# Attention of a two-layer hybrid trunk: looped jobs with f32 value matmuls against one unrolled pipeline with probabilities in two parts

## What is computed

```
# layer 0: 8 latent heads (mla, 96-dim keys) and 8 forgetting heads (fox, bias F[t] - F[s]), all causal
p = softmax(q @ k.T * scale + bias, masked s <= t);  o = p @ v
# layer 1: dilated heads, 3 groups (d1, d4, d16: window / dilation 128/1, 512/4, 2048/16) x 4 heads
lse_g = logsumexp(logits_g);  o_g = softmax(logits_g) @ v_g
o = sum_g softmax_over_groups(lse_g) * o_g          # the merge
# layer 1: 4 sparse heads, three branches on the same queries
o = gate0 * cmp(63 compressed keys) + gate1 * sel(causal here, top 16 of 16 blocks) + gate2 * win(512 back)
mix = concat(o) @ w_out
```

## Time and profile before

| | us |
|---|---|
| median of 3 runs (3382.21 to 3389.79) | 3389.16 |
| profiled execution: span | 3393.3 |
| its own time beside the span | none is recorded apart; the span stands for it, 4.1 above the median |
| TensorE busy (share of the span) | 3124.6 (92%) |
| VectorE busy | 1348.8 (40%) |
| GpSimd busy | 809.7 (24%) |
| ScalarE busy | 727.8 (21%) |
| mean granted clock of TensorE, of full speed | 0.937 |
| first attention, first score to first output projection | 297.5 to 692.8 |
| second attention | 1991 to 2444.1 |

### The profile page before, as it was taken

The page is one execution under the profiler, slowest core; times in us unless marked ns, Lnnn a source line. Parts: engine busy times, 40 slices in busy tenths (PEclk is TensorE's granted clock), DMA queues, the critical chain, the costliest instruction groups (busy, mean ns, idle before and its releaser), DMA issues.

```text
span 3393.3 us, 46007 instructions
## 1 busy us (share of the span) xinstructions
PE 3124.6 (92%) x14660; PEld 2555.4 (75%) x14660; DVE 1348.8 (40%) x2457; ACT 727.8 (21%) x1197; POOL 809.7 (24%) x466
## 2 busy tenths in 40 slices
PE   8897988898999999999999986688889999999999
PEld 5776888875888888876788875577758888888867
DVE  4634554505222222226433148876443222222254
ACT  2203433313100111113210022233331111111131
POOL 2330021321332332322233202100113233233222
PEclk9998987898999999999999986777799999999999
DMA  4236411100111111110135263344101111111101
GB/s 158 107 118 186 104 47 37 49 31 25 50 45 49 49 44 49 49 56 31 38 117 210 79 163 92 88 102 102 44 25 44 50 49 43 49 49 43 62 32 75
DMA packets 69611, 241.10 MB, mean 71 GB/s; under 512 B 9091, under 2 KB 12675, under 8 KB 68663
## 3 DMA queue, kind: packets, MB, share of 16 engines
q1 hardware_dynamic: 57992, 196.35, 19.4%
q10 hardware_dynamic: 11488, 43.16, 3.3%
HBM read 195.60 MB, written 48.59 MB: 72 GB/s over the span
## 4 chain that ended last, share of the span: by engine, by line
PE 79%; DVE 11%; issue 4%; ACT 3%; DMA 2%; SPq 0%; DVEq 0%; ACTq 0%; POOL 0%; POOLq 0%
PE ACC L895 59%; PE OP L1070 7%; PE ACC L1030 5%; PE TR L1045 4%; PE OP L951 3%; DVE R L1487 2%; DVE T L1510 1%; DVE H L1513 1%; DVE XL L1493 1%; PE TR L1082 1%; DVE T L1535 1%; ACT PT L1293 1%; DVE HL L1538 1%; DMA BIASD<-b_d 1%; ACT T L1267 1%
## 5 line engine op out<-in xcount | busy, mean ns | idle before, releaser
L792 POOL CAST WH<-RAW 128x1024 fp32r<-128x1024 f32 x203 | 215.8, 1063 | 1946.1 <-PE ACC L895 1755.7
L895 PE MATMUL ACC<-XH,WH 128*128 128x512 f32 x1792 | 581.6, 406 | 52.4 <-DVE XL L1493 38.4
L895 PE MATMUL ACC<-XL,WH 128*128 128x512 f32 x1792 | 556.8, 392 | 0.0
L895 PE MATMUL ACC<-XH,WL 128*128 128x512 f32 x1792 | 555.7, 391 | 0.0
L794 POOL TENSOR_TENSOR WL<-RAW,WH 128x1024 fp32r<-128x1024 f32 x203 | 495.4, 2440 | 24.2
L895 PEld LDWEIGHTS ACC<-XH,WH 128*128 128x128 f32 x1792 | 337.9, 190 | 158.8 <-issue 75.9
L895 PEld LDWEIGHTS ACC<-XL,WH 128*128 128x128 f32 x1792 | 338.9, 189 | 71.7
L895 PEld LDWEIGHTS ACC<-XH,WL 128*128 128x128 f32 x1792 | 338.7, 189 | 71.8
L1542 DVE TENSOR_TENSOR M<-M,ACC 128x1024 f32<-128x1024 f32 x128 | 156.3, 1221 | 520.8 <-PE ACC L895 520.8
L895 PE MATMUL ACC<-HH,WH 128*128 128x512 f32 x1024 | 322.2, 396 | 17.0 <-DVE HL L1538 17.0
L1265 ACT ACTIVATE HH<-T 128x1024 fp32r<-128x1024 f32 x64 | 68.0, 1062 | 1168.5 <-DVE T L1535 1168.5
(11 more groups left out here) (188 smaller groups left out, 3339.9 us busy)
## 6 DMA issues: line engine op xcount, KB each, us to landing
RAW<-in_w SPq DMA_DIRECT2D x203, 512.0 KB, 3.2
QK<-y_odds SPq DMA_DIRECT2D x128, 256.0 KB, 5.1
y_odds<-HALVES ACTq DMA_DIRECT2D x16, 1024.0 KB, 5.0
QK<-y_foxs SPq DMA_DIRECT2D x48, 256.0 KB, 5.6
y_foxs<-HALVES ACTq DMA_DIRECT2D x8, 1024.0 KB, 4.7
y_kv<-Q ACTq DMA_DIRECT2D x8, 512.0 KB, 2.6
BIAS<-y_f SPq DMA_DIRECT2D x4, 1024.0 KB, 8.3
y_odd<-HALVES ACTq DMA_DIRECT2D x8, 512.0 KB, 2.6
```

The source lines that it names most:

```text
L792: nc.gpsimd.tensor_copy(WH[:, slot], RAW[:, slot]).then_inc(s_whi, 1)
L895: mm = nc.tensor.matmul(acc[:, h * HALF:(h + 1) * HALF], w(k), x[:, k, h * HALF:(h + 1) * HALF], start=first and k == k0 and w is ws and x ...
```

## The change

The attention of each layer becomes one straight line of steps through all its jobs, without loops: `EVEN_JOBS` (4 fox, 4 mla jobs of two heads) and `ODD_JOBS` (d1, d4, d16, cmp of pair 0, the same of pair 1, then sel, win, sel, win). The lags of two and three steps stay. In it:

- A turned group is made into two fp32r parts. For the first four blocks of a task (kind A) ScalarE copies hi and VectorE subtracts lo from `TR`; for the rest (kind B) ScalarE copies to `PTF` and GpSimd makes hi and lo. `PT` now holds two such parts for a chunk of two tasks (256 queries).
- `VS` holds hi and lo of V side by side, 64 columns each, and is the stationary operand; `PT` moves, 256 queries wide. The result is feature rows of V-hi and V-lo, for four tasks (a half) in one `OP` bank. ScalarE copies the lo rows to `CORR`, VectorE adds them and multiplies by the inverse sums, which a matmul of a broadcast column with the identity has turned into a row (`norm`). Transposes of the output go; GpSimd makes `XH` and `XL` (for sel and win it adds the branches too).
- Dilated heads spread sum and extreme over 64 rows with the same matmul. The merge is 14 pieces, one in each step after the last dilated half.
- Mla heads are padded pairs of the same form; the split of Q and K is four pieces in the steps of blocks 2 to 5 (`split_head`).
- Small tasks (dilated, cmp) have four banks of scores and eight of probabilities, the others two and three.
- Room for this is H's: it is overwritten in attention, stored ahead of the second one (`y_h`, eight stores in the gate stage) and loaded back behind each (`reload_h`). SP and ScalarE wait for all stores of the stage before, ahead of the first job; CMPMASK is loaded first in the second attention. Each head's bias is loaded by itself.

```diff
+EVEN_JOBS = [("fox", p) for p in range(4)] + [("mla", p) for p in range(4)]
+ODD_JOBS = ([(k, 0) for k in DILATED] + [("cmp", 0)] + [(k, 1) for k in DILATED] + [("cmp", 1)]
+            + [("sel", 0), ("win", 0), ("sel", 1), ("win", 1)])
...
+        for s in range(len(ts) + VALUE_LAG + 2 + MERGE_PIECES):
+            st = Phase()
+            st.logits, st.turn, st.values, st.norm, st.out, st.start = get(s), get(s - TURN_LAG), None, None, None, None
+            if st.logits and st.logits.first_of_head and st.logits.e == 0:
+                st.start = st.logits.job
+            ended = get(s - VALUE_LAG)
+            if ended and ended is ended.chunk.tasks[1]:
+                st.values = ended.chunk
+                if ended.chunk.closes:
+                    st.norm = ended.chunk.half
+            st.out = ph.steps[-1].norm if ph.steps else None
+            st.merge = [(p, s - s0) for p, s0 in merging if 0 < s - s0 <= MERGE_PIECES]
+            if st.out and st.out is st.out.job.halves[-1] and st.out.job.kind == "d16":
+                merging.append((st.out.job.pair, s))
+                ph.merged[st.out.job.pair] = st.out.no + 1
+            st.split = None
...
+        def group_free(eng, g):
+            if g.seq > 2:
+                x = pt_groups[g.seq - 3]
+                if x.kind == "A":
+                    eng.wait_ge(s_ptD, x.d)
+                else:
+                    eng.wait_ge(s_ptA, x.a)
...
+                def split_turned(t):
+                    c = t.chunk
+                    m = c.tasks.index(t)
+                    for g in t.groups:
+                        if g.kind != "B":
+                            continue
+                        k0 = t.blocks[0] - c.k0 + g.first
+                        hi, lo = (PT[:, c.buf, hl, k0:k0 + g.n, m * P:(m + 1) * P] for hl in range(2))
+                        src = PTF[:, (g.b - 1) % 2, 0:g.n * P].rearrange("p (k q) -> p k q", q=P)
+                        pool.wait_ge(s_ptA, g.a)
+                        wait(pool, s_pv, c.no - 1)
+                        nc.gpsimd.tensor_copy(hi, src).then_inc(s_pth, 1)
+                        pool.wait_ge(s_pth, g.b)
+                        nc.gpsimd.tensor_tensor(lo, src, hi.bitcast(F32), ALU.subtract).then_inc(s_ptB, 1)
...
+                def spread_sums(h):
+                    c0 = h.tasks[0].col
+                    pool.wait_ge(s_exp, h.tasks[-1].no + 1)
+                    wait(pool, s_nrm, h.no - 1)
+                    nc.gpsimd.tensor_copy(PTF[:, h.no % 2].rearrange("p (t m f) -> p t m f", t=4, m=2),
+                                          NML[:, :, c0:c0 + 4].rearrange("p m t -> p t m").unsqueeze(3)
+                                          .to_broadcast([P, 4, 2, HD])).then_inc(s_rl, 1)
...
+                def values(c):
+                    j, col = c.job, c.c % 2 * 256
+                    pe.wait_ge(s_ptD, c.d)
+                    wait(pe, s_ptB, c.b)
+                    if c.opens:
+                        wait(pe, s_o, c.half.no)
+                    order = sorted(c.keys, key=lambda x: x[1] - x[2])
+                    for n, (k, c0, c1) in enumerate(order):
+                        for hl in range(2):
+                            v, pt = VS[:, j.slot, k, c.e * P:(c.e + 1) * P], PT[:, c.buf, hl, k - c.k0, c0:c1]
+                            if j.kind == "cmp":
+                                v, pt = VCS[:, c.e * P:(c.e + 1) * P], PT[0:HD, c.buf, hl, 0, c0:c1]
+                            mm = nc.tensor.matmul(OP[:, 0, col + c0:col + c1], v, pt,
+                                                  start=c.opens and n == 0 and hl == 0,
+                                                  stop=c.closes and n == len(order) - 1 and hl == 1,
+                                                  skip_group_check=True)
+                    mm.then_inc(s_pv, 1)
...
+                def norm(h):
+                    pe.wait_ge(s_rl, h.rl)
+                    wait(pe, s_o, h.no)
+                    wait(pe, s_cor, h.cor_before)
+                    for m, t in enumerate(h.tasks):
+                        if h.job.kind in DILATED:
+                            rows = PTF[:, h.no % 2, m * P:(m + 1) * P]
+                        else:
+                            rows = RL[:, t.col:t.col + 1].to_broadcast([P, P])
+                        mm = nc.tensor.matmul(OP[:, 1, m * P:(m + 1) * P], rows, IDENT[:], start=True, stop=True)
+                    mm.then_inc(s_nrm, 1)
...
+                def correction(h):
+                    rows, other = rows_of_head(h.e), rows_of_head(1 - h.e)
+                    act.wait_ge(s_pv, h.chunks[1].no + 1)
+                    wait(act, s_o, h.no)
+                    nc.scalar.activation(CORR[rows], OP[other, 0], ACT.Copy).then_inc(s_cor, 1)
+                    if h.job.kind in DILATED:
+                        act.wait_ge(s_nrm, h.no + 1)
+                        if h.job.kind == "d1" and h is h.job.halves[0]:
+                            wait(act, s_ox, h.job.pair)
+                        dst, src = by_token(h, DL[rows, DILATED.index(h.job.kind)], OP[HD:P, 1])
+                        nc.scalar.activation(dst, src, ACT.Copy).then_inc(s_cor, 1)
...
+                def turned(t):
+                    c = t.chunk
+                    m, r = c.tasks.index(t), HD if t.kind == "cmp" else P
+                    for g in t.groups:
+                        act.wait_ge(s_tr, g.seq)
+                        src = TR[0:r, g.ring, 0:g.n * P]
+                        if g.kind == "B":
+                            wait(act, s_ptB, g.b - 2)
+                            nc.scalar.activation(PTF[:, (g.b - 1) % 2, 0:g.n * P], src, ACT.Copy).then_inc(s_ptA, 1)
+                            continue
+                        k0 = t.blocks[0] - c.k0 + g.first
+                        wait(act, s_pv, c.no - 1)
+                        nc.scalar.activation(PT[0:r, c.buf, 0, k0:k0 + g.n, m * P:(m + 1) * P],
+                                             src.rearrange("p (k q) -> p k q", q=P), ACT.Copy).then_inc(s_ptA, 1)
...
+            def reload_h(name, src):
+                end = phases[name].end
+                act.wait_ge(s_tr, end.turned)
+                act.wait_ge(s_ttr, end.tasks)
+                wait(act, s_ptB, end.b)
+                wait(act, s_ops, end.ops)
+                if name == "odd":
+                    act.wait_ge(s_ox, 2)
+                for c in range(DC):
+                    act.dma_start(H[:, c], src[c]).then_inc(s_hre, 16)
...
+                def low_turned(t):
+                    c = t.chunk
+                    m, r = c.tasks.index(t), HD if t.kind == "cmp" else P
+                    for g in t.groups:
+                        if g.kind == "B":
+                            continue
+                        k0 = t.blocks[0] - c.k0 + g.first
+                        hi, lo = (PT[0:r, c.buf, hl, k0:k0 + g.n, m * P:(m + 1) * P] for hl in range(2))
+                        dve.wait_ge(s_ptA, g.a)
+                        V_.tensor_tensor(lo, TR[0:r, g.ring, 0:g.n * P].rearrange("p (k q) -> p k q", q=P),
+                                         hi.bitcast(F32), ALU.subtract).then_inc(s_ptD, 1)
...
+                def outputs(h):
+                    j, rows = h.job, rows_of_head(h.e)
+                    dve.wait_ge(s_cor, h.cor)
+                    if j.kind in DILATED:
+                        g = DILATED.index(j.kind)
+                        if j.kind == "d1" and h is j.halves[0]:
+                            wait(dve, s_ox, j.pair)
+                        dst, src = by_token(h, DU[rows, g], OP[rows, 0])
+                        _, cor = by_token(h, DU[rows, g], CORR[rows])
+                        V_.tensor_tensor(dst, src, cor, ALU.add)
+                        dst, src = by_token(h, DM[g][rows], OP[0:HD, 1])
+                        V_.tensor_copy(dst, src).then_inc(s_o, 1)
+                        return
+                    cols = slice(h.h * HALF, (h.h + 1) * HALF)
+                    dst = XF[rows, j.chunk, cols]
+                    if j.kind in ("sel", "win"):
+                        wait(dve, s_xl, h.xl_before)
+                        dst = O[rows, cols]
+                    if j is ph.jobs[-1] and j.kind == "mla" and h.no % 4 == 0:
+                        dve.wait_ge(s_ops, j.ops[1])
+                    V_.tensor_tensor(dst, OP[rows, 0], CORR[rows], ALU.add).then_inc(s_o1, 1)
+                    dve.wait_ge(s_o1, h.o1)
+                    dve.wait_ge(s_nrm, h.no + 1)
+                    V_.tensor_tensor(dst, dst, OP[rows, 1], ALU.mult).then_inc(s_o, 1)
...
+                def merge(p, k):
+                    n = MERGE_STEPS * p
+                    if k == 1:
+                        dve.wait_ge(s_o, ph.merged[p])
+                        V_.tensor_tensor(DMIN[:], DM[0][:], DM[1][:], ALU.min).then_inc(s_md, 1)
+                    elif k == 2:
+                        dve.wait_ge(s_md, n + 1)
```

(14 more changed lines are left out.)

998 lines of the change are left out of this document (465 added, 533 removed).

## The result

The changed kernel takes 3464.8 us (median of 4 runs, 3462.0 to 3469.4) against 3385.7 of the kernel before (4 runs): **1.0239 times the time, 95% interval 1.0222 to 1.0256, 79 us slower**, where 76 us less were forecast. The profiled span is 3462.3 us. The mean granted clock is 0.938, as before.

What follows compares the result with a forecast made beforehand. Gaps and merges, more than the steady heads, were taken as what could be won: 34.4 us in the first attention and 41.8 in the second, 76.2 off 3393.3, gave 3317.1 us profiled, 3313 as median; range 3224 to 3375.

Steps and rivals of the forecast that it cites:

- their 58 matmuls in 10 us: Large heads: argument against a falling clock, since 61 matmuls in 10 us had shown 1.00 and new heads have 58.
- Work of 16.2 and 0.4 for signals: Fox head: 128 TensorE records take 16.2 us, the many more signals 0.4, within 22.0 us a head.
- Matmuls of 256 columns at 0.112 us: Value matmuls, 256 queries wide: taken at 0.112 us each; at 0.16, 1.5 us more a head.
- Denominators 0.9 a half: New denominator rows on TensorE: 8 f32 matmuls, 16 records a head at 0.112 us; 0.9 us in the tail.
- Place one: T6 behind the next head's L0: TensorE waits 2.3 us for VectorE's low part, queued behind score and output passes.
- Place two: The 16 value matmuls after L2: TensorE waits 2.1 us for ScalarE's copies and GpSimd's cast and subtraction.
- Place three: First values of a head after L4: TensorE waits 1.0 us for VectorE's score pass, outputs and low part.
- the clock falls inside the heads: Rival, 0.12: TensorE's pauses lower the clock, some 11 us more per head at 1.2 GHz; 3389 us and up.
- waits of 0.5 and 1.8: Four d1 tasks: values wait twice for the low part, beside 4.2 us of TensorE work; 6.0 us forecast.
- small tasks win nothing: Rival, 0.18: TensorE stays at 1.2 GHz, 48 tasks take 100 us, both merges show in full; 3361 us.
- the prediction's second way: Merge: VectorE's DL products meet GpSimd's DU products even in pieces, so it costs 25 us; uncontended 15.
- the 5.6 and 11.2 given: First attention's bias load: 5.6 us as it is halved, or 11.2 if the 1.5 MB beside it held it.

Runs made afterwards that it cites:

- run 3: Values four steps behind the scores instead of three, nothing else, against the changed kernel: 3340.6 us, 0.9857 of the kernel before.
- run 4: Changed kernel with 128x512 matmuls of no use ahead of the scores of blocks 0 and 2 in fox and mla heads: 3452.9 us.
- run 11: On run 3, the merge passes work on 8 columns of 1024, leaving nearly all of the merge out; one execution: 3312.4 us.
- run 8: On run 3, one more wait: GpSimd begins its merge products only after VectorE's ten two-input passes: 3328.8 us, 0.9843 of the kernel before.

## Why the prediction was wrong

Its sum against the profile (us):

| term | forecast | measured | off |
|---|---|---|---|
| first score | 292 | 295.97 | +4 |
| first attention, first score to first output matmul (710.56) | 366.4 | 414.6 | +48.2 |
| between the attentions, to the second's first score (2014.47) | 1307.2 | 1303.9 | -3.3 |
| two dilated groups | 152 | 200.4 | +48.4 |
| two compressed jobs and merges | 36 + 44 | 97.9 | +17.9 |
| selected, window, filling and tail | 170.3 | 200.5 | +30.2 |

That is 145 of the 152 us by which the forecast missed; the rest is how the profiled executions stand to the medians (4.1 below the span taken, 2.5 above it measured).

**The large heads, the step that failed: a price list without the clock.** The prediction priced TensorE's work at full clock all through the heads, and took their 58 matmuls in 10 us as the reason. Work of 16.2 and 0.4 for signals: right (16.5 here, 16.9 in run 3). Matmuls of 256 columns at 0.112 us: right in short bursts (eight in 0.88 at 406.30 in the chain), 0.13 in bursts of sixteen (2.08). Denominators 0.9 a half: right at full clock (0.94 at 407.18), 1.78 behind a pause (397.60). Place one 2.3: measured 2.4. Place two 2.1: 7.4 / 4 = 1.85. Place three 1.0: 5.0 / 4 = 1.25. Missed were the transposes of V, which at the start of each pair take place one's buffer and wait 2.9 instead: 6.4 us of waits a head for 5.4. The other 2.55 us are the clock. Two mla heads took 51.1 us (bursts at 601.64 and 652.78 in the chain), 25.6 each for 22.6, at a clock of 0.93. The rival "the clock falls inside the heads" had 0.12, and its price, 11 us for a whole head at 1.2 GHz, was the wrong form of it: the clock fell in short pieces in nearly every head. My argument against it, a mean density of matmuls like that of a window at full clock, says nothing on pauses of 2.4 us between bursts; run 4 is the test of it. That waits of 2.3 us are "far shorter" than those after which the rows showed 0.50 was true, and no evidence that they are harmless. The Trainium skill (TensorE: Matmul & The Clock Gate, HAM oscillation — how this bites in real kernels), whose rule I weighed there and set aside, pointed the right way: the rows at 412 us agree that TensorE is put back to the lower clock between short bursts. The waits in its own example are 3 to 5 us long; that 2.4 were enough is shown by this trace alone.

**The dilated jobs, the same step.** Forecast were 6.0 us for four tasks (its own terms, 4.2 of work and waits of 0.5 and 1.8, add up to 6.5), and 76 us for a group, 6.3 for four tasks with what that leaves to the clock. Measured: 200.4 / 24 = 8.3. In the first group TensorE is idle 99.4 - 73.7 = 25.7 us, 2.1 for four tasks, where 2.3 were forecast. It is busy for 6.1 at a mean clock of 0.67; that is 4.1 at full clock (an estimate, busy time by mean clock), where 4.2 were forecast. So work and waits were right, and by this estimate the 2 us between 6.1 and 4.1 are the clock. Run 3's first group comes out the same way: 65.5 x 0.76 / 12 = 4.2 of work, 1.6 idle. The waits have one link more than the prediction named: in d4 and d16 the two strided passes (1.06 and 1.05 us) ahead of the low part wait for ScalarE's copy of the sums (1.11), and this for the denominators, 2.02 us at half clock. The rival "small tasks win nothing" (0.18) had the number, 100 us for a group (99.4 and 101.0), and half of the cause: TensorE stood at 1.2 GHz for two thirds of the first group, not for all of it, and was idle for a quarter. Its merges did not show in full.

**The clock and the 79 us.** That the clock explains the miss does not say that it made the kernel slower than the one before. Over the whole span it costs at most (1 - 0.938) x 3462 = 215 us, and (1 - 0.937) x 3393 = 214 before: the same. What made it slower stands in TensorE's idle time: busy 3124.6 of 3393.3 us before and 3075.6 of 3462.3 now, it has 49 us less of busy and 118 more of idle time. Run 3 took both down: its clock costs at most 0.045 x 3340 = 150, so up to 65 of its 124 us are the clock, and the others are not.

**Compressed jobs and merge:** that pieces lengthen tasks was right; 22 us was too much for the merge (12 in run 11, with four steps), 18 too little for the job by itself (32); what makes up the 32 was not looked into beyond run 11. The contention came as the prediction's second way had it: the products of DL take 3.02 us beside GpSimd's (3.03 in run 3), and 1.21 in run 8, where only a wait was added; even 128x4 elements took 1.91 beside them. The trace agrees with the rule that the prediction cites from the Trainium skill (SBUF — State Buffer, Who interferes with whom). I should have seen that they can be kept apart.

**Selected and window jobs:** the same heads, the same miss: 30 us for eight, 3.8 each, at a clock of 0.87.

**Start, middle and tail:** the bias landed in 7.7 us, between the 5.6 and 11.2 given. The tail of the first attention, last burst at 700.61 to first output matmul at 710.56, is 10 us against 7.6 + 2.1 of values. These were right.

**What was asked of the profile:** waits at L1141 and L1158 came, heads at 25.5 were named as "wrong if at 25", the clock was not 0.95. The one thing that I never priced is the lag itself. I took three steps as given, priced each wait behind it, and did not ask whether one step more would hide it; it was worth 124 us, more than any other run here.

Open stays how much of the dilated jobs' 85 us in run 3 would go at full clock and how much lies with which link of the loop of waits, and whether output passes cut in two or a second `OP` bank would win the 3.7 us of waits left in a large head; that was not tried.

## What to carry to other kernels

When a change puts one more engine, or one more pass, between two TensorE steps, count the new chain from the transpose to the value matmul and widen the lag by it before judging the change: here one step turned 2.4% slower into 1.4% faster. Price a pause of TensorE at its length plus the slower work behind it, even at 2 us, if the pauses keep coming; and price the work of a stage at the clock that its rows show. Inside a step start the longest chain first, and leave a full step between the pass that empties a bank and the matmul that refills it; where GpSimd and VectorE both have passes with two SBUF inputs, one wait that keeps them apart can pay.

## What the runs showed of the hardware

- Pauses of 2.4 us (2.39 ahead of 412.43) were followed by stretches at 0.50 of full clock in the fox heads; work of no use in the pauses brought the clock from 0.90 to 0.97 and made the kernel 12 us faster.
- In the dilated jobs the same raised the clock from 0.76 to 0.95, and the group took 4 us longer: the added matmuls were some 21 us of work (an estimate), more than the clock and the filled waits gave back.
- A VectorE product of 128x1024 with both inputs in SBUF took 3.03 us beside GpSimd's products and 1.21 with these kept behind it (runs 3 and 8, medians of six).
- A VectorE pass of 4 columns with both inputs in SBUF (L1757) took 1.91 us beside GpSimd's product at 2138.79, and 0.17 without one at 2150.80.
